# Head 1's last two key blocks projected inside head 0's backward state loop, in a hybrid token-mixer kernel

## The reference

```python
z = h @ p['w_in']                       # queries, keys, values, gates
qk = silu(dwconv(z[..., :2 * ML_WIDTH], p['ml_conv']))
C_loc = einsum('bhnl,bhnld,bhnle->bhnde', w, v, k)     # one matrix for each chunk of 128 tokens
def step(carry, inp):                   # scan over chunks, forward and backward
    C_new = a[..., None, None] * C + s[..., None, None] * Cl
...
S = einsum('bhntd,bhnsd->bhnts', q, k) * exp(D - m[..., None])
num = einsum('bhnts,bhnsd->bhntd', S, v) + wi * einsum('bhnde,bhnte->bhntd', C0, q)
```

## Time and profile before

| | |
|---|---|
| median of 3 runs | 2568.42 us (2568.36 to 2571.45) |
| the profiled execution | 2571.05 us, span 2569.3 us |
| PE busy | 95% of the span |
| DVE, ACT, POOL busy | 69%, 40%, 24% |
| mean granted TensorE clock | 0.977 |

### The profile page before, as it was taken

How to read it: one execution, slowest core, us unless ns; L and a number is a source line. 1 busy time by engine, 2 the same in 40 slices (tenths; PEclk the granted TensorE clock), 3 DMA queues, 4 the chain that set the end, 5 groups by cost and what they waited for, 6 DMA issues and landing times.

```text
span 2569.3 us, 39429 instructions
## 1 busy us (share of the span) xinstructions
PE 2428.6 (95%) x14652; PEld 1348.2 (52%) x14652; DVE 1767.5 (69%) x3076; ACT 1029.6 (40%) x2020; POOL 624.0 (24%) x512
## 2 busy tenths in 40 slices
PE   6899999998999999989997899999999999999997
PEld 2455655644686868665543344444444444444443
DVE  4874465678885748475677889888987565555665
ACT  3843434657343424242545444454423322222212
POOL 1465438000010101040335354434430000000020
PEclk8999999999999999989998999999999999999999
DMA  8422322100100010051245444454438433333322
GB/s 245 138 76 82 123 75 83 23 24 9 30 18 19 11 26 10 10 148 42 67 176 188 156 149 164 168 174 142 156 111 318 146 98 104 99 107 103 99 70 66
DMA packets 176454, 260.25 MB, mean 101 GB/s; under 512 B 21320, under 2 KB 90952, under 8 KB 175608
## 3 DMA queue, kind: packets, MB, share of 16 engines
q1 hardware_dynamic: 171656, 240.95, 29.7%
q0 software_dynamic: 4608, 16.78, 2.0%
HBM read 179.18 MB, written 78.50 MB: 100 GB/s over the span
## 4 chain that ended last, share of the span: by engine, by line
PE 70%; issue 14%; DVE 7%; ACT 5%; POOL 2%; DMA 2%; SPq 1%; DVEq 0%; POOLq 0%; ACTq 0%
PE pb L3006 20%; PE pb L3105 17%; PE pb L334 13%; PE pb L2991 3%; PE pb L3120 3%; PE pb L2941 2%; PE pb L343 1%; POOL MS L1732 1%; DVE arena L2423 1%; DVE arena L2505 1%; PE pb L300 1%; PE pb L2810 1%; DMA arena<-in_ada_w 1%; PE pb L2904 1%; PE pb L2730 1%
## 5 line engine op out<-in xcount | busy, mean ns | idle before, releaser
L3006 PE MATMUL pb<-arena 128*128 128x512 f16 (+2 forms) x2760 | 594.1, 377 | 28.2 <-DVE arena L2471 17.9
L3105 PE MATMUL pb<-arena 128*128 128x512 f16 x2352 | 513.0, 379 | 0.7 <-DVE arena L2505 0.5
L3006 PEld LDWEIGHTS pb<-arena 128*128 128x128 f16 x2760 | 268.5, 99 | 349.1 <-issue 32.7
L334 PE MATMUL pb<-arena 128*128 128x512 f16 (+1 forms) x1944 | 410.8, 373 | 8.7 <-ACT arena L1232 3.8
L3105 PEld LDWEIGHTS pb<-arena 128*128 128x128 f16 x2352 | 229.4, 98 | 280.1 <-DVE arena L2505 6.3
L2505 DVE SCALAR_TENSOR_TENSOR arena<-pb,arena 128x512 f32<-128x512 f32 x432 | 293.0, 685 | 47.9 <-PE pb L3105 24.7
L334 PEld LDWEIGHTS pb<-arena 128*128 128x128 f16 x1944 | 190.9, 99 | 226.4 <-issue 17.2
L1552 ACT ACTIVATE pb<-pb 128x512 f32<-128x512 f32 x192 | 111.7, 582 | 221.8 <-DVE pb L2476 119.7
L1796 POOL TENSOR_TENSOR arena<-arena 128x512 f32<-128x512 f32 x8 | 13.4, 1699 | 496.0 <-DVE arena L2505 496.0
L1761 POOL TENSOR_TENSOR arena<-arena 128x1024 f32<-128x1024 f32 x32 | 81.0, 2553 | 212.8 <-DMA arena<-in_mlp_w 212.8
L343 PE MATMUL pb<-arena 128*128 128x128 f16 x2016 | 123.9, 221 | 6.8 <-ACT arena L1326 4.9
(11 more groups left out here) (366 smaller groups left out, 4019.1 us busy)
## 6 DMA issues: line engine op xcount, KB each, us to landing
w1x<-arena SPq DMA_DIRECT2D x112, 256.0 KB, 2.1
arena<-w1x SPq DMA_DIRECT2D x112, 256.0 KB, 2.7
w2x<-arena SPq DMA_DIRECT2D x106, 256.0 KB, 2.1
arena<-w2x SPq DMA_DIRECT2D x106, 256.0 KB, 2.8
arena<-in_x SPq DMA_DIRECT2D x128, 128.0 KB, 4.1
arena<-in_ada_rest POOLq DMA_DIRECT2D x32, 512.0 KB, 3.9
arena<-in_mlp_w SPq DMA_DIRECT2D x64, 256.0 KB, 6.2
arena<-in_mlp_w SPq DMA_DIRECT2D x16, 1024.0 KB, 5.6
```

The source lines that it names most:

```text
L334: mm = pe.matmul(pb[:, bank(jb, b), 0:n], whl[:, (i + 1) % 2, KT * ws + k, :], hT[:, k, hs, t0:t0 + n], start=(k == 0 and m == 0), stop=(k ...
L3006: mm = pe.matmul(pb[:, up_bank(pas, s, j), c], (lo if ws else hi)[:, k, :], token_op(b, L // 2, c)[:, k, hs, :], start=(k == 0 and m == 0) ...
L3105: mm = pe.matmul(pb[:, 4 + at % 4, :], left[:, hs, P * tt:P * tt + P], right[:, ws, :], start=(e == 0 and m == 0), stop=(e == 1 and m == 2))
```

## The change

`k1` is projected only up to block 2 ahead of the loop. Blocks 3 and 4 are projected by a new function, `project_part`, between the backward states: three matmuls of 512 columns after each `csum` for x = 0 to 7 (block 3), four matmuls of 256 columns for x = 8 to 13 (block 4). ACT's copies of the two blocks move from ahead of the loop to behind `kw` of x = 8 and of x = 14. DVE's, POOL's and SP's instructions keep their order.

```diff
+        def project_part(pe, jb, b, first, last):
+
+            i, u, n = jb["i"], unit(jb, b), BLK if b < NB else TC
+            steps = [(kt, ws, hs) for kt in range(KT) for ws, hs in ((0, 0), (0, 1), (1, 0))]
+            if first == 0:
+                pe.wait_ge(S("w_split"), i + 1)
+                pe.wait_ge(S("p_ev"), u - 1)
+            for x in range(first, last):
+                kt, ws, hs = steps[x]
+                mm = pe.matmul(pb[:, u % 2, 0:n], whl[:, (i + 1) % 2, KT * ws + kt, :], hT[:, kt, hs, BLK * b:BLK * b + n],
+                               start=(x == 0), stop=(x == len(steps) - 1))
+            if last == len(steps):
+                mm.then_inc(S("p_mm"), 1)
@@ -1404,8 +1418,6 @@
                     act.activation(ZM[:, 0:L], QT, ACT.Tanh, scale=0.5).then_inc(S("m_th"), 1)
-                    parked_keys(3)
-                    parked_keys(4)
                     act.wait_ge(S("m_silu"), 2 * h + 2)
@@ -1426,6 +1438,8 @@
+                    if h == 0 and x in (8, 14):
+                        parked_keys(3 if x == 8 else 4)
                     if h == 0 and x == 10:
                         split_hi(act, jq["i"] + 2)
@@ -2855,7 +2869,7 @@
                 if h == 0:
-                    project(pe, J["k1"])
+                    project(pe, J["k1"], range(3))
@@ -2914,6 +2928,10 @@
                     csum(i0 + x, seq[x])
                     if h and x < 12:
                         value_chunk(2 - x // 4, x % 4)
+                    if h == 0 and x < 8:
+                        project_part(pe, J["k1"], 3, 3 * x, 3 * x + 3)
+                    if h == 0 and 8 <= x < 14:
+                        project_part(pe, J["k1"], 4, 4 * x - 32, 4 * x - 28)
```

## The result

| | before | change |
|---|---|---|
| median of 10 runs each | 2570.15 us (2565.48 to 2572.15) | 2573.92 us (2571.17 to 2579.56) |
| ratio | | 1.0020, 95% interval 1.0011 to 1.0028 |
| profiled execution's span | 2569.3 us | 2572.2 us |
| PE busy | 2428.6 us, 95% | 2426.0 us, 94% |

The change makes the kernel 3.8 us slower by the medians and 5.1 us (0.20%) by the ratio, interval 2.8 to 7.2 us. So it is slower, if by little: the interval lies wholly above 1. The first three runs of before had their median at 2568.42; ten have it at 2570.15. In the second timings of experiments 5 and 4 one execution each took 5112.64 and 3205.98 us; the ratios leave these two out.

The account below looks back on a forecast made before the run. PE was taken to bound the kernel ahead of the loop, the PE–ACT round trip inside it. 2.0 us at full clock plus 2.2 us of low clock gave +4.2 on 2568.42: 2572.6 us, range 2568.5 to 2577.0.

Parts of the forecast that it names:

- the favoured case: Backward loop of head 0: late start with a low clock and no more, +4.2 us (+3.5 to +4.9), chance 0.55.
- rival 2: Behind the loop: low clock again, 1.7 us on top, +5.9 us, 2574.3 us, slower by a measurable amount; chance 0.27.
- The front gives 3.06 us and no more: Ahead of the loop: 7.78 us leave PE, but `kw` waits for the queries' SiLU, so only 3.06 us is gained.
- PE idle for 5.2 us: Before the first `csum`: PE finishes two `ktr` at 698.4 and idles until 703.59, 5.2 us.
- Rounds of 0.98 and 0.76, loop of 14.39 us at full clock: Backward loop: rounds of 0.98 us for x below 8, 0.76 for x = 8 to 13, against 0.53; PE-bound.
- The split of weights at x = 10: In the loop: hides behind the longer rounds, costed at nothing; without that cover up to 1 us of ACT time.
- Waits at x = 9 and 15 of 0.44 and 0.67 us: In the loop: copies of blocks 3 and 4 on ACT delay `csum`, 0.44 us at x = 9, 0.67 at x = 15.
- The low clock costs 1.5 to 2.85 us, 2.2 taken: First loop rounds: idle PE drops the clock, matmuls take twice as long, 1.5 to 2.85 us lost, mean 2.2.
- The sum of +4.2: Up to `heads(0)`: 2.0 us later at full clock plus 2.2 us for the low clock, +4.2 us.
- The whole delay passes to the end: Behind `heads(0)`: engines follow in order through PE's forward rounds, so all +4.2 us reaches the kernel's end.
- Rival 1: Before the loop: the clock stays up despite idle PE, only +2.0 us, 2570.4 us; chance 0.10.
- Rival 3: In the loop: the parts fit into the waits, rounds stay as long, 3.06 us gained, 2565.4 us; chance 0.08.

Follow-up runs that it names:

- experiment 5: Change, but block 3 projected before the first `csum`, block 4 between `ktr` and waiting `csum`, both copies behind the first forward `kw`: 2567.18 and 2566.83 us, ratios 0.9998, 0.9996.
- experiment 4: Change with only block 4 moved, its matmuls between `ktr` and the waiting `csum`, its copy behind the first forward `kw`: 2566.18 and 2566.11 us, ratios 0.9993, 0.9990.
- experiment 1: Change plus 22 unread matmuls of 512 columns on PE between the second `ktr` and the first `csum` of head 0: 2573.16 us, ratio 1.0015.
- experiment 6: Change with ACT's two copies moved out of the loop, behind the first forward `kw`, PE's order unchanged: 2569.85 us in one run.
- experiment 2: Kernel before, plus unread matmuls of the same number, shapes and places as the change puts into the loop: 2578.09 us in one run.

## Why the prediction was right

The forecast was no measurable change on the slow side, 2572.6 us in 2568.5 to 2577.0, 4.2 us above the median of before. The median came at 2573.92, 3.8 us above the median of the ten runs of before beside it. The steps up to `heads(0)` came out one by one, so the number was not luck there. Two things were less good than it looks. The measurement told a change of 0.2% from none, which the forecast had put at its limit. And the favoured case, a late start with a low clock "and no more", is not what the profiles show: rival 2's second low stretch was there too, and the time can't tell the two sums (4.2 and 5.9 us) apart. Step by step:

- *The front gives 3.06 us and no more.* First `csum` 2.78 us behind the start of the SiLU was worked out; it is 700.31 - 697.56 = 2.75; of the 0.07 us taken between the SiLU's end and `kw`, 0.04 was used (699.85 to 699.89). What the trace of one execution could not say is that PE's lag behind DVE varies: from the SiLU's start to the first `ktr` it is 4.94 us in the first profile of before and 4.52, 4.79 and 4.63 in the others, so the front gives 2.7 to 3.1. The execution that the prediction read had the largest value, and the loss is accordingly 0.2 us larger on average (anchors of before 14.93 in the mean, of the change 19.26: 4.3 us).
- *PE idle for 5.2 us.* 5.39.
- *Rounds of 0.98 and 0.76, loop of 14.39 us at full clock.* 14.33 in experiment 1. The load alone: 14.24 measured, 14.2 expected. The split of weights at x = 10 hid as costed: in the change `csum` 11 starts at 713.04, 0.11 us behind its `ktr`.
- *Waits at x = 9 and 15 of 0.44 and 0.67 us.* In the change 711.40 stands 0.23 us after PE could have been there (711.06 + 0.11), where 0.33 was worked out, and the wait at 716.19 is 0.45 in place of 0.56: both 0.1 us too long. Of these 0.2 us only 0.06 is left in the sum of the loop (14.39 against 14.33), since other small terms were too short; that part of the agreement is luck. The copies themselves are worth 0.1 us (experiment 6).
- *The low clock costs 1.5 to 2.85 us, 2.2 taken.* 16.46 - 14.33 = 2.1 us. The low clock lasted 4.4 us from the restart, which was also the mean of the five rows. Two remarks on those rows. In the first the clock fell only 1.0 us behind the restart of 536.67, so it was low for 3.4 us of work and not 4.4; the mean price is then 2.1 us. And the five were a selection: in the same trace PE also stood idle for 2.66, 2.94, 3.32 and 4.52 us (before 117.32, 1131.16, 1335.98 and 1376.93), and behind each of these too the clock was low, for 3.4 us, up to 3.8 or 3.9 us from the restart. Of the Trainium skill, the page "TensorE: Matmul & The Clock Gate", Part 1, has the throttled rate as the default that activity releases. This case's traces agree: 2.1 us lost behind 5.39 us of idleness, and none in experiment 1.
- *The sum of +4.2.* 19.21 - 15.15 = 4.06 between the SiLU and `heads(0)` in the two profiles compared, 4.3 by the means.
- *The whole delay passes to the end.* The medians (3.8 us) and the ratio's interval (2.8 to 7.2 us) agree with that and don't prove it; the spans of single executions scatter too much behind `heads(0)` (7.3 us over the fourteen profiles) to show it.
- *Rival 1 (the clock stays up)* is what experiment 1 had to build by force. *Rival 2* had its mechanism: the second low stretch was there in both profiles of the change. Its price of 1.7 us was half of 3.4 us; it costs 1.1. Part of the rest may hide in waits: with the clock up, PE waits 0.30 us for DVE in that place (before 722.89 in the kernel before), which is not there in the change. No run separates it further. With it the loss up to the first gate projection was 4.1 + 1.1 = 5.2 us in the profile compared, between the forecast's 4.2 and rival 2's 5.9, and so is the ratio's 5.1. The low clock in head 1 that this rival was read from began at 834.6, not 834.4; nothing hangs on it. *Rival 3* was excluded by PE's work, and experiment 2 measured it: 4.9 us longer for 7.8 us put in. What the loop takes for nothing was shown for the 2.6 us of block 4 standing in the waits (experiment 4); that it would take all 3.9 us of its gaps was not tried.

## What to carry to other kernels

Work that fills a wait must stand inside it: between the instruction that starts the other engine's turn and the one that waits for it. The same 24 matmuls cost 1.4 us behind `csum` (with a copy on ACT in the loop that is worth at most 0.2 of it) and nothing between `ktr` and `csum`. And before work is taken away from ahead of a wait, look at what ends that wait: here DVE's SiLU gave 3 us of the 7.8, and the rest became idle PE that brought on the low clock, so that even matmuls nobody reads made the way up to `heads(0)` 2 us shorter.

## What the runs showed of the hardware

- TensorE's clock fell 3.0 and 3.1 us into an idle stretch and came back 4.4 and 4.6 us after the restart in the two profiles of the change, at a cost of 2.1 and 2.2 us of a loop in which PE was the bound.
- The stretch of short waits behind the loop had the low clock in ten of fourteen profiles. The kernel before and the one of experiment 5 were each seen both with and without it: some 1.1 us of difference between executions of one kernel from this place alone.
- The part of the program behind `heads(0)` took 1848.8 to 1856.1 us over the fourteen profiles; a change of some us here can only be priced between events close to it.
